# Projections of the first block as three fp32r products, weights split in halves, and the modulation sums on GpSimd

## The reference, cut to what matters

```python
h = rms_norm(x, norm_gain)
proj = h @ w_in                      # 1024 x 10240
(sb_q, sb_k, sb_v, sb_g, r_q, r_k, r_v, r_g, m_sb, m_ret) = split(proj)
out_a = stick_breaking_attention(rms(sb_q), rms(sb_k), sb_v) * silu(sb_g)   # 8 heads of 128
out_b = rms(chunkwise_retention(rotary(r_q), rotary(r_k), r_v)) * silu(r_g) # 4 heads of 256
merged = sigmoid(m_sb + b0) * (out_a @ w_branch_sb) + sigmoid(m_ret + b1) * (out_b @ w_branch_ret)
x = x + merged @ w_out
```

## Time and profile before

| | |
|---|---|
| median of three runs | 1717.01 us (1713.64 to 1721.86) |
| profiled execution, its own time | 1718.75 us |
| its span, first to last instruction | 1717.4 us, mean granted PE clock 0.970 |
| PE busy | 1634.0 us, 95% |
| DVE, ACT, POOL busy | 889.3 us (52%), 534.0 us (31%), 416.0 us (24%) |
| first block, steps 0 to 30 | 14.0 to 261.1 us |
| steps 31 to 39 | 262.05 to 341.19 us |
| merge, to the end of its last out part | 341.19 to 435.9 us |

### The profile page before, as it was taken

The page is one execution under the profiler, slowest core; times in us unless marked ns, Lnnn a source line. Parts: engine busy times, 40 slices in busy tenths (PEclk is TensorE's granted clock), DMA queues, the critical chain, the costliest instruction groups (busy, mean ns, idle before and its releaser), DMA issues.

```text
span 1717.4 us, 24193 instructions
## 1 busy us (share of the span) xinstructions
PE 1634.0 (95%) x9505; PEld 1213.7 (71%) x9505; DVE 889.3 (52%) x1826; ACT 534.0 (31%) x921; POOL 416.0 (24%) x273
## 2 busy tenths in 40 slices
PE   7999999999899977798989999999999999999998
PEld 3444455544455536745889999999999888888886
DVE  3466663231243335343768884333333576767676
ACT  1103221120122222111134434434333444545443
POOL 0000000000000110000088888888888000000000
PEclk9999999999999968798999999999999999999999
DMA  9776753332834480023266566766666477777776
GB/s 320 267 269 214 252 180 114 104 142 98 272 118 150 166 324 2 3 98 127 98 172 148 138 146 139 145 148 137 147 140 145 127 236 238 237 238 237 236 239 211
DMA packets 179525, 297.17 MB, mean 173 GB/s; under 512 B 48763, under 2 KB 94139, under 8 KB 179285
## 3 DMA queue, kind: packets, MB, share of 16 engines
q1 hardware_dynamic: 135688, 285.47, 48.9%
q0 software_dynamic: 36864, 0.15, 5.7%
q10 hardware_dynamic: 6860, 10.01, 1.7%
HBM read 276.55 MB, written 19.03 MB: 172 GB/s over the span
## 4 chain that ended last, share of the span: by engine, by line
PE 92%; DMA 3%; DVE 2%; issue 1%; ACT 1%; POOL 0%; SPq 0%; ACTq 0%; DVEq 0%; POOLq 0%
PE bank L461 31%; PE bank L872 14%; PE bank L870 14%; PE bank L874 14%; PE bank L882 6%; PE bank L852 3%; DMA slot<-in_w_in_dram 2%; PE bank L445 1%; PE bank L728 1%; DMA slot<-in_expert_down_dram 1%; PE bank L479 1%; PE bank L739 1%; PE bank L738 0%; PE bank L676 0%; PE bank L675 0%
## 5 line engine op out<-in xcount | busy, mean ns | idle before, releaser
L461 PE MATMUL bank<-slot,hT 128*128 128x512 f32 (+2 forms) x1088 | 473.4, 592 | 12.6 <-DMA slot<-in_w_in_dram 8.2
L2003 POOL DMA_INDIRECT c_dram<-gates,places x256 | 397.7, 1554 | 202.8 <-DVE gates L1526 125.1
L461 PEld LDWEIGHTS bank<-slot,hT 128*128 128x128 f32 x1088 | 206.2, 193 | 256.0 <-issue 246.2
L870 PE MATMUL bank<-hT_high,dT_high 128*128 128x256 f32 x1024 | 297.9, 291 | 0.0
L872 PE MATMUL bank<-hT_low,dT_high 128*128 128x256 f32 x1024 | 289.7, 283 | 0.0
L874 PE MATMUL bank<-hT_high,dT_low 128*128 128x256 f32 x1024 | 287.9, 281 | 0.0
L1438 DVE TENSOR_TENSOR dT_low<-bank,dT_high 128x512 fp32r<-128x512 f32 x256 | 165.0, 686 | 220.1 <-ACT dT_high L1924 219.1
L874 PE MATMUL bank<-up_high,A_low 128*128 128x512 f32 x512 | 202.1, 395 | 0.0
L870 PE MATMUL bank<-up_high,A_high 128*128 128x512 f32 x512 | 201.6, 394 | 0.4 <-DVE A_low L1438 0.4
L872 PE MATMUL bank<-up_low,A_high 128*128 128x512 f32 x512 | 200.7, 392 | 0.0
L874 PEld LDWEIGHTS bank<-hT_high,dT_low 128*128 128x128 f32 x1024 | 194.2, 190 | 0.0
(11 more groups left out here) (394 smaller groups left out, 1603.0 us busy)
## 6 DMA issues: line engine op xcount, KB each, us to landing
slot<-in_expert_down_dram SPq DMA_DIRECT2D x128, 512.0 KB
slot<-in_expert_up_dram SPq DMA_DIRECT2D x128, 512.0 KB, 3.4
slot<-in_w_in_dram SPq DMA_DIRECT2D x27, 2048.0 KB, 8.1
P<-in_w_ada_dram SPq DMA_DIRECT2D x24, 1024.0 KB, 5.5
c_dram<-zeros SPq DMA_DIRECT2D x1, 16384.0 KB, 50.5
slot<-c_dram SPq DMA_DIRECT2D x128, 128.0 KB, 3.3
slot<-in_w_out_dram SPq DMA_DIRECT2D x4, 2048.0 KB, 7.9
slot<-in_w_query_dram SPq DMA_DIRECT2D x4, 2048.0 KB, 8.0
```

Of the source, the lines that this page charges most:

```text
L461: m = pe.matmul(sums, lhsT=lhs[:, k, t * P:(t + 1) * P], rhs=w[:, k, :], start=(k == 0), stop=(k == w.shape[1] - 1))
L870: pe.matmul(o, lhsT=lhs_high.bitcast(F32R), rhs=rhs_high.bitcast(F32R), start=start, stop=False, skip_group_check=True)
L2003: g.indirect_dma_start(C_dram, bass.IndirectOffsetOnAxis(ap=places[:, x, k:k + 1], axis=0), gates[:, x, k:k + 1], None, compute_op=ALU.add ...
```

## The change

- **Three products.** The 26 chunks of the first block and its merge are multiplied by `pe_three`. `h`, and later the transposed attention outputs and merged tokens, are kept as high and low parts (`h_hi`, `h_lo`, `oa_hi`, `oa_lo`).
- **Halves.** These chunks come as 52 halves of 512 rows (1 MB). ACT copies each into an fp32r high part (`a_split`), DVE subtracts in place (`v_split`): the low part takes the slot's own place. Half h may be asked for when PE has used half h-4; there are three, later four buffers for high parts. In step x PE now multiplies half x with both token tiles; the splits of half x+2 stand first in step x of ACT's queue and in the middle of DVE's. Sums of chunk c are taken out in step 2c+2.
- **Modulation pieces on POOL.** A new `g_first_block` makes the low part of `h` and then all 24 pieces: a multiply of the whole piece with `cs` broadcast along the columns, and three adds that halve it. SP asks for pieces at fixed halves, the last, piece 23, ahead of half 30; rows are summed by PE at the ends of steps 5, 7, 9, 12, 15, 16, 19, 21, 23, 25, 28 and 30.
- **In the merge** the splits of halves 42 to 51 stand between the parts of the queues; the bias of the gates is added as chunks 16 to 19 are taken out (`v_project`), and its two 128x2048 additions go; the square of the retention output moves to step 39.
- The gain and bias for the merge are loaded in step 28 instead of step 1. The scatter's semaphores are fewer and counted on. Buffers lie elsewhere in SBUF.

```diff
+    ADA = 6 * D // AW
+    row_step = [5, 7, 9, 12, 15, 16, 19, 21, 23, 25, 28, 30]
+    row_at = {x: r for r, x in enumerate(row_step)}
+    ada_load = {int((6 + 8 * (p - 1)) / 6.9 + 3.99): p for p in range(2, ADA)}
+    ada_b_load = {row_step[r - 2] + 6: r for r in range(2, ADA // 2)}
+    assert len(ada_load) == ADA - 2 and len(ada_b_load) == ADA // 2 - 2
+    SPLIT = 26
...
+    w_high_at = {h: h % 3 for h in range(40)}
+    w_high_at.update({40 + n: (1, 2, 0, 3)[n % 4] for n in range(12)})
...
+    def half_used(eng, h):
+        if h % 2:
+            held(eng, (*chunks[h // 2][0], 0, 1))
+        else:
+            eng.wait_ge(half_done, h // 2 + 1)
...
+    def pe_halves(name, hi, lo, t, halves):
+        i = chunk_at[name]
+        key = (*name, 0, t)
+        if halves[0] == 0:
+            b = block_next[0]
+            block_next[0] = (b + 1) % 4
+            fill(key, b)
+        sums = bank[psum.at[key][0]]
+        for half in halves:
+            h = 2 * i + half
+            pe.wait_ge(w_low_made, h + 1)
+            for k in range(KT // 2):
+                at = (slice(None), half * KT // 2 + k, slice(t * P, (t + 1) * P))
+                m = pe_three(sums, lo[at], hi[at], w_low[h % 4][:, k, :], w_hi[w_high_at[h]][:, k, :],
+                             half == 0 and k == 0, half == 1 and k == KT // 2 - 1)
+            if half:
+                m.then_inc(filled(key), 1)
+            elif t == 1:
+                m.then_inc(half_done, 1)
...
-            pe_block(("in", x // 2), hT, x % 2)
+            if x < 2:
+                pe.wait_ge(h_split, 2 * x + 2)
+            for t in range(TT):
+                pe_halves(("in", x // 2), h_hi, h_lo, t, (x % 2,))
             pe_ada_row(x)
...
-                pe_block(("sb", c), oaT, t)
+                if c == 0:
+                    clear(pe, ("oaT", 2 * t))
+                    clear(pe, ("oaT", 2 * t + 1))
+                pe_halves(("sb", c), oa_hi, oa_lo, t, (0, 1))
         pe.wait_ge(ret_done, 1)
         pe_turn("obT", tiles_of(ret_o))
-        for k in range(4):
-            clear(pe, ("obT", k))
         for c in range(2):
             for t in range(TT):
-                pe_block(("ret", c), obT, t)
+                if c == 0:
+                    clear(pe, ("obT", 2 * t))
+                    clear(pe, ("obT", 2 * t + 1))
+                pe_halves(("ret", c), h_hi, h_lo, t, (0, 1))
...
-    def v_ada_sum(x):
-        if x in ada_at:
-            p = ada_at[x]
-            r = p // 2
-            acc, w = ada_acc[r % 2][:, p % 2 * AW:(p % 2 + 1) * AW], ada_w[p % 2]
-            v.wait_ge(ada_in[p % 2], 16 * (r + 1))
-            if r > 1:
-                held(v, ("ada", r - 2))
-            v_own.settle(v.tensor_scalar(acc, w[:, 0, :], cs[:, 0:1], None, ALU.mult))
-            for k in range(1, KT):
-                m = v.scalar_tensor_tensor(acc, w[:, k, :], cs[:, k:k + 1], acc, ALU.mult, ALU.add)
-                if k < KT - 1:
-                    v_own.settle(m)
-            m.then_inc(ada_summed, 1)
...
+    def v_split(h):
+        v.wait_ge(w_high, h + 1)
+        v_low(w_low[h % 4], half_view(h), w_hi[w_high_at[h]]).then_inc(w_low_made, 1)
+
+    def v_turn_split(tag, hi, lo, n):
+        for k in range(4):
+            b = held(v, (tag, k))
+            at = (slice(None), slice(k % 2 * 4, k % 2 * 4 + 4), slice(k // 2 * P, (k // 2 + 1) * P))
+            v.wait_ge(turn_high, 4 * n + k + 1)
+            v_low(lo[at], b.rearrange("p (k n) -> p k n", k=4), hi[at]).then_inc(emptied((tag, k)), 1)
...
-            v_ada_sum(x)
+            v_split(x + 2)
+            if x % 2 == 0 and x:
+                c = x // 2 - 1
+                for t in range(TT if c > 15 else 1):
+                    v_project(c, t)
...
+        v_split(42)
         v_rstd(stat[:, 32:40], stat[:, 32:40], (ret_rooted, 1))
         for t in range(TT):
             o = ret_o[:, t].rearrange("p (h d) -> p h d", h=RET_H)
             m = v.tensor_tensor(o, o, ret_s[:, t].unsqueeze(2).broadcast_to([P, RET_H, RET_D]), ALU.mult)
         v_own.settle(m)
         v.tensor_tensor(ret_o, ret_o, P1[:, :, RG, :], ALU.mult).then_inc(ret_done, 1)
+        v_split(43)
+        v_split(44)
         v.wait_ge(merge_gated, 2)
-        for c in range(2):
+
+        def sb_part(c):
             for t in range(TT):
                 v_gated(("sb", c, 0, t), c, t, lambda t, at: P1[:, t, M1, at], merged1, None, aside1, aside_free)
-        v_turn("obT", by_tile(obT, KT), 4)
-        for c in range(2):
+
+        def ret_part(c):
             for t in range(TT):
                 v_gated(("ret", c, 0, t), c, t, lambda t, at: P1[:, t, M2, at], aside1, merged1, aside1, None)
-        v_turn("mT", by_tile(hT, KT), 4)
+
+        sb_part(0)
+        v_split(45)
+        v_split(46)
+        v_turn_split("obT", h_hi, h_lo, 1)
+        sb_part(1)
+        v_split(47)
+        v_split(48)
+        ret_part(0)
+        v_split(49)
+        v_split(50)
+        ret_part(1)
+        v_turn_split("mT", oa_hi, oa_lo, 2)
+        v_split(51)
...
+    def a_split(h):
+        a.wait_ge(half_in[h % 4], 16 * (h // 4 + 1))
+        used = [g for g in range(h) if w_high_at[g] == w_high_at[h]]
+        if used:
+            half_used(a, used[-1])
+        a.copy(w_hi[w_high_at[h]].bitcast(F32R), half_view(h)).then_inc(w_high, 1)
...
+        a_split(42)
+        a_split(43)
+        for t in range(TT):
+            for c in range(16, 20):
+                clear(a, ("in", c, 0, t))
             a.activation(P1[:, t, M1:M2 + 1, :], P1[:, t, M1:M2 + 1, :], ACT.Sigmoid).then_inc(merge_gated, 1)
-        clear(a, ("reto", 1, 0))
-        clear(a, ("reto", 1, 1))
-        a.activation(ret_sq, ret_o, ACT.Square).then_inc(ret_squared, 1)
         a.wait_ge(ret_summed, 1)
         a_root(stat[:, 32:40], stat[:, 32:40], RET_D, 1, ret_rooted)
-        for c in range(2):
-            a_take(("sb", c, 0, 1), aside1[:, 1, c * CW:(c + 1) * CW])
-        a_turn("obT", by_tile(obT, KT), 4)
-        for c in range(2):
-            a.wait_ge(aside_free, c + 1)
-            a_take(("ret", c, 0, 1), aside1[:, 1, c * CW:(c + 1) * CW])
-        a_turn("mT", by_tile(hT, KT), 4)
+        a_split(44)
+        a_split(45)
+        a_take(("sb", 0, 0, 1), aside1[:, 1, 0:CW])
+        a_split(46)
+        a_turn_split("obT", h_hi)
+        a_split(47)
+        a_take(("sb", 1, 0, 1), aside1[:, 1, CW:])
+        a_split(48)
+        a_split(49)
+        a.wait_ge(aside_free, 1)
+        a_take(("ret", 0, 0, 1), aside1[:, 1, 0:CW])
+        a_split(50)
+        a.wait_ge(aside_free, 2)
+        a_take(("ret", 1, 0, 1), aside1[:, 1, CW:])
+        a_turn_split("mT", oa_hi)
+        a_split(51)
...
+    def g_first_block():
+        for n, (t, k) in enumerate(((0, 0), (1, 0), (0, 1), (1, 1))):
+            at = (slice(None), slice(4 * k, 4 * k + 4), slice(t * P, (t + 1) * P))
+            g.wait_ge(h_rounded, 2 * t + k + 1)
+            g.tensor_tensor(h_lo[at].bitcast(F32R), hT[at], h_hi[at], ALU.subtract).then_inc(h_split, 1)
+        g.wait_ge(silu_done, 1)
+        for p in range(ADA):
+            r = p // 2
+            acc, w = ada_acc[r % 2][:, p % 2 * AW:(p % 2 + 1) * AW], ada_w[p % 2]
+            g.wait_ge(ada_in[p % 2], 16 * (r + 1))
+            g_own.settle(g.tensor_tensor(w, w, cs.unsqueeze(2).broadcast_to([P, KT, AW]), ALU.mult))
+            for k in (4, 2):
+                g_own.settle(g.tensor_tensor(w[:, 0:k, :], w[:, 0:k, :], w[:, k:2 * k, :], ALU.add))
+            if r > 1:
+                held(g, ("ada", r - 2))
+            g.tensor_tensor(acc, w[:, 0, :], w[:, 1, :], ALU.add).then_inc(ada_summed, 1)
...
+    def s_halves():
+        for h in range(2 * SPLIT):
+            if h in ada_load:
+                s_ada(ada_load[h])
+            if h in ada_b_load:
+                s_ada_b(ada_b_load[h])
+            if h > 3:
+                half_used(sp, h - 4)
+            name, w, c0, n = chunks[h // 2]
+            rows = slice(h % 2 * D // 2, (h % 2 + 1) * D // 2)
+            sp.dma_start(half_view(h), w[rows, c0:c0 + n].rearrange("(k p) n -> p k n", p=P)).then_inc(half_in[h % 4], 16)
+            if h in (1, 2):
+                s_ada(h - 1)
+            if h == 3:
+                s_ada_b(0)
+                s_ada_b(1)
```

More of the change, by code:

```diff
@@ L137, in program @@
     SB, RET = [14 + 4 * i for i in range(4)], [30, 34]
-    ada_step = [x for x in range(2, 30) if x % 7 != 6]
-    ADA = len(ada_step)
-    assert ADA == 6 * D // AW
-    ada_at = {x: p for p, x in enumerate(ada_step)}
-    row_at = {ada_step[2 * r + 1] + (2 if r == 6 else 1): r for r in range(ADA // 2)}
+    ADA = 6 * D // AW
[5 more added lines that the diff above has]
+    SPLIT = 26
+    half_in, half_done = [sem(f"half{j}_in") for j in range(4)], sem("half_done")
+    w_high, w_low_made = sem("w_high"), sem("w_low_made")
+    h_rounded, h_split, turn_high = sem("h_rounded"), sem("h_split"), sem("turn_high")
```

(58 more changed lines are left out.)

108 lines of the change are left out of this document (52 added, 56 removed).

## The result

The changed kernel takes 1736.12 us (median of 4 runs, 1732.88 to 1736.35), the kernel before 1716.61 us (4 runs on the same chip). The ratio is 1.0106, 95% interval 1.0078 to 1.0133: **slower by 1.1%**, 19.5 us. The forecast was 1748 us, slower by 1.8%, with a range from 1695 to 1780.

The account below looks back on a forecast made before the run. PE bounded the kernel before; after, POOL's pieces and DVE's two-input instructions sharing one interface would pace the first block. 39 - 11.8 + 2 + 0.3 + 1.3 = 31 us on a 1717.4 us span: 1748 us, range 1695 to 1780.

Parts of the forecast that it names:

- the upper bound: First block: POOL waits for the whole duration of a DVE two-SBUF-input instruction, 2.29 us per subtraction; lower bound nothing.
- Rival A: First block: POOL isn't held up by DVE; last row at 224.5 instead of 301.2, 1669 us; chance 0.18.
- forecast 223: First block: PE alone, without POOL's delay, would come to the last modulation row, end of step 30, at 223 us.
- the like case: POOL's piece multiply, scaled from the earlier row with one broadcast input: 3.6 us, against 4.5 by plain-input rows.
- The interface term: First block: POOL's 198 us and DVE's 84 share one interface from 18 us; done at 300, +39 us at last row.
- whoever wins each turn: First block: POOL's and DVE's whole durations add to 282 us; if POOL always won, DVE would be equally late.
- Rival B: First block: POOL held only in part, a third to two thirds of 84 us hidden; 1692 to 1720 us; chance 0.10.
- The step that failed was SP's: First block: SP's queue stays behind POOL; piece, half and splits take some 15 us, less than two slowed pieces' 23.5.
- stalls of 4, 6 and 12 us: Merge: PE waits at the retention root, before ret and before out; merge 95 us against 94.7.
- 3 us for it: Merge: 3 us added for PE's lower clock after the three stalls.
- +2 us for the clock in steps 31 to 39: Steps 31 to 39: PE returns at the lower clock after standing about 10 us before step 31, +2 us.
- +1.3 us at the second block: After the merge: second block's first chunk is asked for one shorter part closer to its use, +1.3 us.

Follow-up runs that it names:

- the experiment with one input: Changed kernel with DVE's subtraction of each half replaced by a same-size reduction with one SBUF input (products wrong): 1695.53 us.
- without pieces: Changed kernel with the multiply and first two adds of each modulation piece left out of POOL's loop (values wrong): 1675.72 us.
- the half asked for first: Changed kernel with SP asking for each modulation piece one place later, behind the half it stood before: 1734.61 us.
- its other order: Changed kernel with the merge's splits put behind the root and gated parts on ACT and DVE, nothing left out: 1714.3 us, ratio 0.9984.

## Why the prediction was right, and where it was off

**The side and the mechanism were right.** POOL is held by DVE for whole instructions, which no row of before showed and for which the forecast took the upper bound. The Trainium skill states it for this pair of forms ("SBUF — State Buffer", section "SBUF: two separate sides": whichever starts first has the shared pair of ports for its whole instruction); the trace agrees in both directions, with 5.65 us against 3.60 and 5.21 against 2.29. Rival A is out: the row comes at 286.96, not 224.5, and the experiment with one input shows that A is the world in which DVE's instruction has one. The prices of its parts were sound too: without pieces the last row starts at 223.4 (forecast 223), the multiply is 3.60 us (the like case of the earlier trace rows, not the 4.5 us of the plain ones), steps 31 to 39 give 12.3 us (11.8).

**The interface term was too large by 22 us.** The forecast: start at 18, 198 of pieces, 84 of DVE's, done at 300. After: start at 21.94 (+3.9, most of it from h's low part, 2.18 us a quarter instead of 1.26), 195.3 of pieces with their gaps (24 x 7.94 = 190.6, and 257.3 - 252.6 = 4.7 of gaps; -2.7), and 62.0 held (252.6 - 190.6; -22.0): done at 279.2. The experiment with one input puts 57.0 of the 62.0 on the subtractions, 1.84 us for each of 31, where I had counted 2.29. The timeline shows the larger part of the difference. Of the 24 multiplies 12 took 5.65 or 5.66 us and 12 took 3.59 to 3.61, none anything between: a held one lost 2.05 us. The ten held adds of 128x1024 took 4.27 to 4.34 us against 2.34, so 1.93 to 2.00 more. So 0.24 to 0.36 of a subtraction's 2.29 us ran in the gap before POOL's next instruction or while that one started, 7 to 11 us over 31 of them, out of 14; the rest I can't place. The other 5.0 us (195.6 - 190.6) are norms, masks and rotation, for which I had 12.9. They too are two-input instructions, but it is they who mostly lose (2.61 us against 0.68). The step that was mis-sized is the sum of whole durations, "whoever wins each turn": it leaves no part of a DVE instruction to run while POOL isn't reading. Rival B named this (POOL's setup, or its waiting, inside DVE's instruction), but with 28 to 56 of the 84 us hidden; 22 were, and at 31 it has the change break even.

**The step that failed was SP's.** "A piece and a half then the two splits are some 15 us, less than the 23.5 us that two slowed pieces take." The 15 us came out, from 259.27 to 274.6 is 15.4, though with some luck: the load took 8.5 us, not the 10.8 of a piece and a half, and the held subtraction 4.98, not 2.29. But behind them, before the row, stand DVE's copies and masks, PE's attention matmuls and a block, 12.3 us more (274.64 to 286.96; until 282.4 PE's matmuls there still start 0.43 us apart). I compared the load and the splits with POOL's two pieces and left out what follows the splits: 27.7 us in all against the 20.3 that POOL took from 258.86 to 279.2. The row ended 8.6 us after POOL's last add instead of 1.2. With the half asked for first that distance was 2.0 (POOL's last add done at 281.45, the row at 283.45).

So 301.2 - 22.0 - 2.7 + 3.9 + 7.4 = 287.8, the end measured. Two errors, of 22 and 7.4 us, partly cancelled, and the merge's 5.4 us, below, took back more: that the time came within 12 us of the forecast owes something to luck.

**The merge was worse than forecast by 5.4 us.** PE's waits there:

```profile
PE bank L468 <- DVE P L1169: 9.3, 1, 9.3
PE bank L489 <- DVE w_low L1018: 6.5, 1, 6.5
PE bank L489 <- DVE h_lo L1018: 6.1, 1, 6.1
```

They sum to 21.9 us. The forecast's stalls of 4, 6 and 12 us are, by its own times and less the 1.8 of transposes in the last, 3.8, 6.4 and 10.3 us of waiting, 20.5 in all. The first is 2.7 longer, the others (6.1, and the 9.3 before mT's transposes) 0.3 and 1.0 shorter. The first: half 43 was taken as landed, but it is asked for when half 39 has been used, which is the end of step 39. The chain shows it:

```profile
354.75 5.01 DMA slot<-in_w_branch_sb_dram
...
361.70 1.28 ACT L1824
...
373.20 2.29 DVE w_low L1018
375.53 0.80 PE bank L489
376.33 0.43 PE bank L491
```

ACT's second copy waits for that load (3.06 us), and the root with it. The forecast itself had the rule ("a half can only be asked for when the one four before is used") and applied it to halves 46 and 50 only. What the merge lost beside the waits is seen by its other order, which has the same instructions: PE is busy for 78.46 us there in the change and for 71.70 in the experiment. The 6.8 us between them are the clock. Behind a wait, fp32r matmuls of 512 columns start 0.43 us apart, the 1.2 GHz level, instead of the 0.23 of the earlier trace rows, from 376.33 to 381.02 and from 394.55 to 398.3, and behind the third wait the 16 transposes take 3.67 us instead of 1.97, the first matmuls after them again start 0.43 apart. From the distances between starts that is 2.7, 1.8, 1.7 and 0.6 us, 6.8 in all. The window's mean granted clock is 0.86, against 1.00 in the other order. The forecast had 3 us for it, and 71.2 us for PE's work (91.7 less the 20.5) where the experiment shows 71.7. So 3.8 of clock, 0.5 of work and 1.4 of waits make the difference, within the 0.3 us by which the forecast was rounded up. The term that was mis-sized most is thus the clock's.

**What was cost and didn't come.** +2 us for the clock in steps 31 to 39: their granted clock is 1.00, since PE had worked through the whole block of step 30 before. +1.3 us at the second block: its first chunk was indeed asked for 6.3 us before the merge's end instead of 7.6, and PE stood 0.5 us there; but the wait of the earlier trace rows is for the chunk after it, which both kernels ask for as the merge ends (455.21 and 436.02 us) and which took 8.3 and 8.4 us to land. That wait was 2.1 us instead of 2.91.

## What to carry to other kernels

Before giving GpSimd work beside VectorE, count the two-SBUF-input instructions that each issues in the same stretch: their durations come close to adding up (62 of 84 us here), and a split of one job between the two can be worth less than leaving it whole on VectorE (1672.6, 1689.5, 1695.4 us with 0, 6 and 12 of 24 pieces moved, the loads where they were). When a sum frees a buffer whose load stands in a common queue, carry the path on past the load to the consumer (load, copies, attention, block: 27.7 us here) before calling it shorter than the producer's cycle. New work put in a serial chain, as the splits in the merge, goes behind what the next matmul needs: order alone was worth 25 us in the merge, and by the two ratios (1.0106 and 0.9984) some 21 us of the kernel's time.

## What the runs showed of the hardware

- The hold goes both ways and takes whole instructions; the number of SBUF inputs decides. A DVE reduction of 128x2048 from one input left POOL's multiply at 3.61 us, a subtraction of two made it 4.63 in the mean, which is 12 times 5.65 and 12 times 3.60: held for 2.05 us or not at all.
- POOL's multiply of 128x2048 with one input broadcast along the innermost dimension takes 3.60 us, its plain add of 128x1024 2.34.
- A DVE TENSOR_SCALAR of 128x256 from SBUF, with one tensor input, took 1.02 us in the mean beside POOL, 0.34 us without: I had counted only instructions with two. Its like with its input in PSUM (`sb_T`) kept 0.47. The Trainium skill ("SBUF — State Buffer", section "Who interferes with whom") has tensor_scalar among the instructions that can take both ports; this row agrees with it, though none here separates that from waiting for the one before it.
- A load of 1 MB that stood alone in SP's queue took 5.0 us, one queued behind another of the same size 8.5 us.
- Three waits of 6.5, 6.1 and 9.3 us in the merge cost 6.8 us more in matmuls and transposes at the lower level of PE's clock; waits of 2.2, 0.8 and 0.8 us in the other order left its granted clock at 1.00.
